# Six slots of raw weights instead of two in a decoder step's first block, on one Trainium2 core

## The chip, the cores and the metric

The kernel runs on one core of one Trainium2 chip. The metric is device time in microseconds (us), the median of several executions. The engines are named as in the profile: PE (TensorE, matmuls), PEld (its weight loads), DVE (VectorE), ACT (ScalarE), POOL (GpSimd) and SP (SyncE, which here only issues DMAs). ACT and POOL issue DMAs too.

## The reference

One inference step of a decoder block for a prompt of 2048 tokens and 8 decode tokens, all in f32, width 1024:

```python
mp, pc, pC, pn, pm = hybrid_mixer(rmsnorm(hp, g_mix[l]), zc, zC, zn, zm, w_in[l], ..., w_out[l], chunk_p)
hp = hp + mp
pk, pv = mem_kv(mem_prompt, g_mem[l], w_xkv[l])
hp = hp + cross_attn(rmsnorm(hp, g_cross[l]), pk, pv, w_xq[l], w_xo[l])
hp = hp + swiglu(rmsnorm(hp, g_ffn[l]), w_gu[l], w_down[l])
...
y_prompt = rmsnorm(hp, g_final)
```

`hybrid_mixer` is a large input projection, a short convolution, a recurrence over chunks (mLSTM) and an output projection; `mem_kv` makes keys and values of a memory of 256 rows; the FFN has width 2816. The 8 decode tokens take the same weights with states and caches of their own.

## The kernel before, in words

**Groups of weights.** All weights come as groups, tiles of 128x1024 f32 (512 KB), numbered in the order in which PE uses them. Groups 0 to 15 make the memory's keys and values from 256 columns. Groups 16 to 31 fold those keys and values into the query and output weights; the 32 results (the "made" tiles) go to DRAM as `made_d`. Then come five blocks of tokens, the first of 512, the others of 384, and each block uses the same 121 groups: a gate group, 4 groups for the output gate, 24 for the 4 heads (6 per head), 8 of `w_out`, 16 of cross-attention (from `made_d`), and 68 of the FFN. `G_LOW` = 32 + 121 = 153 is the end of the first block's groups.

**Raw groups.** A matmul is done in three passes over a high and a low part of both operands. Every group below `G_LOW` is raw: SP loads it from DRAM into a slot of `w_raw` (`NR` slots), ACT copies it, rounded, into the high half of a slot of `w_hl` (lines 998 and 1044, `NS` = 6 slots), and then the rest is computed by a subtraction, on DVE for groups 0 to 15 (line 1396) and on POOL for 16 to 152 (lines 477, 482). Of the first block's groups SP stores both halves (1 MB) to `split_d` (line 391); the four later blocks load these 1 MB tiles straight into `w_hl` and have no raw groups.

**The order of the work.** Each engine has its own program, in an order written out by hand, and counts on semaphores tie them together. SP loads the first `NR` groups at the start; after that the load of raw group n is issued when the subtraction of group n - NR is done, behind the store of group n - NR where there is one. ACT's copy of group n waits for its load, for PE to be done with group n - 6 (`group_done`), and for the store of group n - 6. In ACT's program this copy (`w_high`) stands between its other work (evictions from PSUM, exponentials, squares), so what stands behind it waits too.

**The place of the decode tokens' weights.** `dwt`, four slots of 128x1024, is a tensor of its own; POOL loads rows of weights into it in the third and fourth block (`decode_rows`), and PE uses them there for the 8 decode tokens.

Of the kernel before, what the change touches and what calls it, by code (L numbers as in the profile page):

```python
# [12 lines left out]
P = 128  # L13
D = 1024
# [27 lines left out]
G_MEM = 16  # L42
# [17 lines left out]
G_LOW = G_KV + G_BLK  # L60

NS = 6
NP = 3
NR = 2


C_BIN = 0
# [47 lines left out]
def gw(b, off):  # L115

    return G_KV + b * G_BLK + off
# [33 lines left out]
def raw(g):  # L151

    return g < G_LOW
# [8 lines left out]
OUT_COUNT, RAW, STORES, LOADS = [], [], [], []  # L162
# [12 lines left out]
def trunk(nc, x_blk, mem_x, w_kv, w_st, w_dec, cst_d, mats_d, st_conv, st_c, st_n, st_m, kd_d, vd_d,  # L175
          y, o_pconv, o_pc, o_pm, o_mk, o_mv, o_sconv, o_sc, o_sn, o_sm, rows_d, drow_d, vrow_d, qrow_d, prow_d, split_d, made_d):
    with ExitStack() as ctx:
        def sb(name, shape, dt=F32):
            return ctx.enter_context(nc.sbuf_tensor(name, shape, dt))

        def sem(name):
            return ctx.enter_context(nc.semaphore(name))
# [5 lines left out]
        act_lo = sb("act_lo", [P, KT, WM], F32R)  # L188
        w_raw = sb("w_raw", [P, NR, D])
        w_hl = sb("w_hl", [P, NS, 2, D], F32R)  # L190
        w_hi, w_lo = w_hl[:, :, 0, :], w_hl[:, :, 1, :]

        dwt = sb("dwt", [P, 4, D])
        big = sb("big", [P, 8200])
        work = sb("work", [P, 4128])
        V1 = P + 1
# [104 lines left out]
        def sems(names):  # L301
            return [sem(n) for n in names.split()]

        cst_loaded, mats_loaded, x0_loaded, xnext_loaded, x_loaded, set_up, dec_loaded = sems(
            "cst_loaded mats_loaded x0_loaded xnext_loaded x_loaded set_up dec_loaded")
        w_loaded = sems("w_loaded_0 w_loaded_1")
        memx_loaded = sems("memx_loaded_0 memx_loaded_1 memx_loaded_2 memx_loaded_3")

        w_hi_done, w_lo_kv, w_lo_done, group_done, out_a, out_v = sems(
            "w_hi_done w_lo_kv w_lo_done group_done out_a out_v")  # L310
# [59 lines left out]
        def _(sp):  # L370
            def weights(g):
                src = w_kv[g] if g < G_KV else w_st[g - G_KV]
                if attends(g):
                    src = made_d[g - gw(0, O_XQ)]
                i = RAW[g] - 1
                sp.dma_start(w_raw[:, i % NR, :], src).then_inc(w_loaded[i % NR], 16)

# [7 lines left out]
            sp.dma_start(cst[:], cst_d).then_inc(cst_loaded, 16)  # L385
            for g in range(NR):
                weights(g)
# [12 lines left out]
            raws = [g for g in range(G_LOW) if raw(g)]  # L400
            for i in range(NR, len(raws) + NR):
                g = raws[i - NR]

# [33 lines left out]
        def _(pool):  # L437
            def load_rows(b):

                n = tok(b) + BLK[b]  # L440
                pool.wait_ge(rows_stored, b * 32 + 32)
                for h in range(HEADS):
                    pool.dma_start(bc[:, h, 0:n], rows_d[h:h + 1, 0:n].to_broadcast([P, n])).then_inc(bc_loaded, 16)  # L443

            def load_x(b):

                after(pool, y_stored, b * 64)
                for k in range(0, KT, 4):
                    pool.dma_start(x[:, k:k + 4, 0:tok(b)],
                                  x_blk[b * KT + k:b * KT + k + 4, :, 0:tok(b)].rearrange("k p c -> p k c")).then_inc(x_loaded, 16)  # L450
                if b == DO:
                    pool.dma_start(x[:, :, DC:DC + NDEC],
                                  x_blk[DM * KT:DM * KT + KT, :, DC:DC + NDEC].rearrange("k p c -> p k c")).then_inc(x_loaded, 16)

            def load_next(b):

                w = w_mix(b + 1)
                pool.wait_ge(y_lo, b * 8 + 8)
                for k in range(0, KT, 4):
                    pool.dma_start(x_next[:, k:k + 4, 0:w],  # L460
                                  x_blk[(b + 1) * KT + k:(b + 1) * KT + k + 4, :, 0:w].rearrange("k p c -> p k c")).then_inc(xnext_loaded, 16)

            def store_y(b):
                w = w_ffn(b)
                for k in range(0, KT, 2):
                    pool.wait_ge(y_ready, b * 8 + k + 2)
                    pool.dma_start(y[b * KT + k:b * KT + k + 2, :, 0:w].rearrange("k p c -> p k c"),
                                  x[:, k:k + 2, 0:w]).then_inc(y_stored, 16)

            for g in range(G_MEM, G_LOW):  # L470
                if not raw(g):
                    continue
                pool.wait_ge(w_hi_done, RAW[g])
                raw_w, hi_w, lo_w = w_raw[:, (RAW[g] - 1) % NR, :], w_hi[:, g % NS, :], w_lo[:, g % NS, :]
                if g == gw(0, O_GATE):
# [17 lines left out]
            def decode_mixer():  # L493

                pool.wait_ge(drow_stored, 16)
                for h in range(HEADS):
                    pool.dma_start(dbc[:, h, :], drow_d[h:h + 1, :].to_broadcast([P, 24])).then_inc(dbc_loaded, 16)

            def decode_states():
                pool.wait_ge(o_lo, DM * 8 + 8)  # L500
                for h in range(HEADS):
                    pool.dma_start(c_dec[:, h * NDEC:(h + 1) * NDEC, :].rearrange("p t v -> p (t v)"),
                                   st_c[:, h * 1024:(h + 1) * 1024]).then_inc(c_loaded, 16)
                pool.wait_ge(vrow_stored, 16)
                rows = vrow_d.rearrange("(s h t) d -> s h (t d)", s=2, h=HEADS)
                for h in range(HEADS):

                    after(pool, dc_ready, 2 * h - 1)
                    pool.dma_start(k_bc.rearrange("p t d -> p (t d)"), rows[1, h:h + 1, :].to_broadcast([P, NDEC * P])).then_inc(vb_loaded, 16)
                    after(pool, dc_ready, 2 * h)  # L510
                    for i in range(2):
                        src = rows[0, h:h + 1, i * 512:(i + 1) * 512].rearrange("h (e c) -> h e c", c=64).to_broadcast([P, 8, 64])
                        pool.dma_start(q_bc[i], src).then_inc(qb_loaded, 16)
                pool.wait_ge(dc_ready, 2 * HEADS)
                pool.dma_start(o_sc, big[:, 4096:8192]).then_inc(dst_stored, 16)
                pool.dma_start(o_sn, dn).then_inc(dst_stored, 16)
                pool.wait_ge(dy_ready, 1)
                pool.dma_start(o_sconv, dcout.rearrange("p i h t -> p (i h t)")).then_inc(dst_stored, 16)
# [15 lines left out]
            def decode_rows(i):  # L534

                after(pool, dw_used, i - 3)
                pool.dma_start(dwt[:, i % 4, :], w_dec[i] if i < KT else w_kv[G_MEM + i]).then_inc(dw_loaded[i % 4], 16)

            def decode_caches():
                pool.wait_ge(o_lo, DO * 8 + 8)  # L540
                cache(0)
                cache(1)
                pool.wait_ge(qrow_stored, 16)
                for i in range(4 * NDEC):
                    if i == 2 * NDEC:
                        pool.wait_ge(prow_stored, 16)
                    piece_row(i)

                    if i % 2 == 0 and 4 <= i:
                        cache(i // 2)  # L550

            for b in range(1, NB):
                load_rows(b)
                if b == DM:
                    decode_mixer()
                store_y(b - 1)
                load_x(b)
                if b < NB - 1:
                    load_next(b)
                if b == DM:  # L560
                    decode_states()
                if b == DO:
                    for i in range(KT):
                        decode_rows(i)
                    decode_caches()

                    for i in range(4):
                        decode_rows(KT + i)
                if b == DX:
                    for i in range(4, KT):  # L570
                        decode_rows(KT + i)
# [1462 lines left out]
```

## Time and profile before

| | |
|---|---|
| median of 3 runs | 2984.13 us (2983.05 to 2984.96) |
| profiled execution, its own time | 2980.44 us |
| its span, first to last instruction | 2978.6 us |
| PE busy | 2892.0 us, 97% |
| DVE, ACT, POOL busy | 1177.9, 754.5, 427.9 us |
| moved by DMA | 801.14 MB, mean 269 GB/s |

A row of the timeline gives start, duration, engine, line, operation, output tile and inputs, and in brackets how long the engine had been idle and what released it. A window's row gives each engine's busy time, PE's granted clock as a share of full speed, the mean busy share of the 16 DMA engines, and what they moved.

### The profile page before, as it was taken

How to read it: one execution, taken by the hardware profiler on the slowest of the kernel's cores; microseconds unless marked ns; L12 is line 12 of the kernel's file. 1: busy time of each engine (PE TensorE's matmuls, PEld its weight loads, DVE VectorE, ACT ScalarE, POOL GpSimd, SP SyncE). 2: the span in 40 equal slices, each digit the busy share in tenths (PEclk: the TensorE clock that was granted, in tenths of full speed). 3: DMA queues.
4: the chain of work that ended last, by engine and by line, in shares of the span. 5: the costliest groups of instructions: out<-in, count | busy, mean ns of one | idle time of the engine just before them, and what ended most of it. 6: DMA issues, size and time to landing. Idle time of an engine off the chain costs nothing.

```text
span 2978.6 us, 38344 instructions
## 1 busy us (share of the span) xinstructions
PE 2892.0 (97%) x15739; PEld 2706.0 (91%) x15739; DVE 1177.9 (40%) x2240; ACT 754.5 (25%) x1472; POOL 427.9 (14%) x286
## 2 busy tenths in 40 slices
PE   7789999999999999999999999999999999999998
PEld 6667877888889999999997999998899999999998
DVE  5525546422553344323333456533332233332223
ACT  4433334322232231103222110222220123221001
POOL 0543343444420000000000102000000000000000
PEclk9999999999999999999999999999999999999999
DMA  5787686978977777877676789976666777567674
GB/s 185 235 322 265 221 306 225 315 277 280 315 268 277 257 277 278 301 266 289 249 283 253 286 343 371 363 272 247 217 250 244 265 264 277 219 251 249 253 267 178
DMA packets 143974, 801.14 MB, mean 269 GB/s; under 512 B 15949, under 2 KB 31693, under 8 KB 64057
## 3 DMA queue, kind: packets, MB, share of 16 engines
q1 hardware_dynamic: 112048, 719.10, 66.5%
q0 software_dynamic: 16208, 67.87, 6.5%
q10 hardware_dynamic: 15544, 11.72, 1.3%
q8 instruction: 126, 2.06, 0.3%
q14 instruction: 48, 0.39, 0.0%
HBM read 650.30 MB, written 148.33 MB: 268 GB/s over the span
## 4 chain that ended last, share of the span: by engine, by line
PE 85%; DMA 6%; DVE 2%; POOL 2%; ACT 2%; issue 2%; SPq 0%; ACTq 0%; DVEq 0%
PE gb L613 75%; DMA w_raw<-w_st 3%; PE gb L853 3%; POOL w_hl L482 2%; PE ta L853 2%; DMA w_raw<-w_kv 2%; ACT w_hl L998 1%; PE td L853 1%; DMA big<-kd_d 1%; DMA w_raw<-made_d 0%; PE ta L722 0%; PE gm L835 0%; DVE work L1550 0%; PE tb L733 0%; DVE w_hl L1396 0%
## 5 line engine op out<-in xcount | busy, mean ns | idle before, releaser
L613 PE MATMUL gb<-xn_hi,w_hl 128*128 128x384 f32 (+2 forms) x5800 | 1582.8, 349 | 4.4 <-DVE x L1639 1.4
L613 PEld LDWEIGHTS gb<-xn_hi,w_hl 128*128 128x128 f32 x5800 | 1061.0, 188 | 53.2 <-issue 5.3
L613 PE MATMUL gb<-xn_lo,w_hl 128*128 128x384 f32 (+2 forms) x2920 | 1011.9, 347 | 0.0
L613 PE MATMUL gb<-act_hi,w_hl 128*128 128x384 f32 (+3 forms) x3296 | 872.1, 344 | 22.2 <-DVE w_hl L1396 11.2
L613 PEld LDWEIGHTS gb<-act_hi,w_hl 128*128 128x128 f32 x3296 | 599.5, 189 | 55.9 <-DVE w_hl L1396 11.5
L613 PEld LDWEIGHTS gb<-xn_lo,w_hl 128*128 128x128 f32 x2920 | 548.9, 188 | 24.2 <-issue 0.5
L613 PE MATMUL gb<-act_lo,w_hl 128*128 128x384 f32 (+3 forms) x1648 | 564.1, 342 | 0.0
L482 POOL TENSOR_TENSOR w_hl<-w_raw,w_hl 128x1024 fp32r<-128x1024 f32 x136 | 330.2, 2433 | 495.2 <-ACT w_hl L998 495.2
L1447 DVE TENSOR_TENSOR work<-gb,r_res 128x384 f32<-128x384 f32 (+2 forms) x220 | 128.3, 585 | 555.4 <-PE gb L613 522.0
L613 PEld LDWEIGHTS gb<-act_lo,w_hl 128*128 128x128 f32 x1648 | 312.1, 189 | 12.3 <-issue 0.2
L1639 DVE TENSOR_TENSOR x<-x,gb 128x384 f32<-128x384 f32 (+2 forms) x200 | 115.4, 581 | 417.4 <-PE gb L613 414.1
L998 ACT ACTIVATE w_hl<-w_raw 128x1024 fp32r<-128x1024 f32 x147 | 154.6, 1057 | 390.9 <-DMA w_raw<-w_st 157.5
L1298 ACT ACTIVATE work<-work 128x384 f32<-128x384 f32 (+2 forms) x110 | 59.9, 545 | 514.9 <-DVE work L1447 514.8
L1301 ACT ACTIVATE act_hi<-work 128x384 fp32r<-128x384 f32 (+2 forms) x110 | 60.1, 546 | 333.0 <-DVE work L1866 333.0
L1218 ACT ACTIVATE work<-x 128x384 f32<-128x384 f32 (+2 forms) x120 | 65.6, 546 | 309.4 <-DVE x L1639 286.9
L1653 DVE TENSOR_TENSOR r_res<-r_res,work 128x384 f32<-128x384 f32 (+2 forms) x119 | 91.1, 766 | 68.5 <-ACT work L1218 67.0
L443 POOL DMA_DIRECT2D big<-rows_d x20 | 10.9, 551 | 658.5 <-DMA rows_d<-big 658.5
L1866 DVE TENSOR_TENSOR work<-work 128x384 f32<-128x384 f32 (+2 forms) x110 | 85.3, 775 | 28.1 <-ACT work L1298 17.5
L1108 ACT ACTIVATE big<-gb,cst 128x384 f32<-128x384 f32 (+1 forms) x80 | 48.5, 606 | 175.3 <-PE gb L613 173.9
L1549 DVE TENSOR_TENSOR work<-ta,big 128x128 f32<-128x128 f32 x64 | 18.6, 291 | 184.2 <-ACT work L1189 141.6
L1853 DVE TENSOR_TENSOR act_lo<-work,act_hi 128x384 fp32r<-128x384 f32 (+2 forms) x110 | 85.0, 773 | 12.4 <-ACT act_hi L1301 11.7
L853 PE MATMUL gb<-w_hl,xn_hi 128*128 128x512 f32 x240 | 78.0, 397 | 5.8 <-DVE x L1639 5.8
(303 smaller groups left out, 2071.0 us busy)
## 6 DMA issues: line engine op xcount, KB each, us to landing
w_hl<-split_d SPq DMA_DIRECT2D x484, 1024.0 KB, 5.0
split_d<-w_hl SPq DMA_DIRECT2D x121, 1024.0 KB, 5.0
w_raw<-w_st SPq DMA_DIRECT2D x105, 512.0 KB, 5.9
w_raw<-w_kv SPq DMA_DIRECT2D x32, 512.0 KB, 3.7
made_d<-big ACTq DMA_DIRECT2D x32, 256.0 KB, 4.0
w_raw<-made_d SPq DMA_DIRECT2D x16, 512.0 KB, 5.8
big<-kd_d POOLq DMA_DIRECT2D x8, 1024.0 KB, 10.8
big<-vd_d POOLq DMA_DIRECT2D x8, 1024.0 KB, 12.8
```

Source lines behind the costliest of these rows:

```text
L482: pool.tensor_tensor(lo_w, raw_w, hi_w.bitcast(F32), ALU.subtract).then_inc(w_lo_done, 1)
L613: mm = pe.matmul(gb[:, ps, 0:wd], a[:, s, k * P:(k + 1) * P], r[:, k, 0:wd], start=(first and k == ks[0] and i == 0), stop=(last and k == ...
L853: mm = pe.matmul(score_bank(p, t), a[:, kt, t * P:(t + 1) * P], r[:, g % NS, n * 512:n * 512 + 512], start=(kt == 0 and f == 0), stop=(kt ...
L998: act.activation(w_hi[:, n % NS, :], w_raw[:, i % NR, :], ACT.Copy).then_inc(w_hi_done, 1)
L1218: act.activation(sq_res[:, 0:wd], x[:, e, 0:wd], ACT.Square).then_inc(res_sq, 1)
L1298: act.activation(et[:, 0:W], gt[:, 0:W], ACT.Silu).then_inc(e_ffn, 1)
L1301: act.activation(act_hi[:, f, 0:W], ht[:, 0:W], ACT.Copy).then_inc(hid_hi, 1)
L1447: return lambda ps: v.tensor_tensor(dst[:, 0:wd], ps[:, 0:wd], r_res[:, 0:wd], ALU.mult)
L1639: return lambda ps: v.tensor_tensor(x[:, e, 0:wd], x[:, e, 0:wd], ps[:, 0:wd], ALU.add)
L1653: v.tensor_tensor(acc_res[:, 0:wd], acc_res[:, 0:wd], sq_res[:, 0:wd], ALU.add).then_inc(res_acc, 1)
L1853: v.tensor_tensor(act_lo[:, f, 0:W], ht[:, 0:W], act_hi[:, f, 0:W].bitcast(F32), ALU.subtract).then_inc(hid_lo, 1)
L1866: v.tensor_tensor(ht[:, 0:W], et[:, 0:W], ut[:, 0:W], ALU.mult).then_inc(h_ffn, 1)
```

## The change

`NR` goes from 2 to 6. The four new slots take no new memory: `dwt` becomes slots 2 to 5 of `w_raw`. Four more semaphores count the loads. In the third block (`DO`), ahead of the first load of decode rows, POOL waits until the last raw group has been subtracted.

```diff
-NR = 2
+NR = 6
...
-        dwt = sb("dwt", [P, 4, D])
+        dwt = w_raw[:, 2:6, :]
...
-        w_loaded = sems("w_loaded_0 w_loaded_1")
+        w_loaded = sems("w_loaded_0 w_loaded_1 w_loaded_2 w_loaded_3 w_loaded_4 w_loaded_5")
...
                 if b == DO:
+
+                    pool.wait_ge(w_lo_done, RAW[G_LOW - 1] - G_MEM)
                     for i in range(KT):
                         decode_rows(i)
```

SP's program at its start (`w_kv` holds groups 0 to 31, `w_st` those of the blocks, `split_d<-w_hl` are the stores), as a difference of before (-) and the changed kernel (+):

```order
 L385 DMA cst<-cst_d 128x96
-L376 DMA w_raw<-w_kv 128x1024 x2
+L376 DMA w_raw<-w_kv 128x1024 x6
 L388 DMA mats<-mats_d 128x896
-L376 DMA w_raw<-w_kv 128x1024 x30
-L376 DMA w_raw<-w_st 128x1024 x2
-L391 DMA split_d<-w_hl 128x2048
```

Six loads stand ahead of that of `mats` instead of two, and each later load stands four groups earlier against the stores: six loads of the first block's groups, instead of two, are issued before its first store.

SP's program where the raw groups end (`w_hl<-split_d` are the later blocks' loads):

```order
 L391 DMA split_d<-w_hl 128x2048
 L376 DMA w_raw<-w_st 128x1024
-L391 DMA split_d<-w_hl 128x2048 x2
+L391 DMA split_d<-w_hl 128x2048 x6
 L398 DMA w_hl<-split_d 128x2048 x484
```

The last six stores have no load between them, where before it was two. The instructions of PE, ACT, DVE and POOL keep their order.

## Rows read from the trace of the kernel before

**Rows 1.** The page: PE's busy time, and the chain that ended last

```profile
PE 2892.0 (97%) x15739; PEld 2706.0 (91%) x15739; DVE 1177.9 (40%) x2240; ACT 754.5 (25%) x1472; POOL 427.9 (14%) x286
...
PE gb L613 75%; DMA w_raw<-w_st 3%; PE gb L853 3%; POOL w_hl L482 2%; PE ta L853 2%; DMA w_raw<-w_kv 2%; ACT w_hl L998 1%; PE td L853 1%; DMA big<-kd_d 1%; DMA w_raw<-made_d 0%; PE ta L722 0%; PE gm L835 0%; DVE work L1550 0%; PE tb L733 0%; DVE w_hl L1396 0%
```

**Rows 2.** Windows: length, busy time of each engine, PEclk, DMA share, GB/s

```profile
0.00:32.00 32.00, 11.65 (x49) 10.36 (x50) 14.86 (x30) 13.60 (x23) 0.20 (x4) 0.79 0.73 245
32.00:77.00 45.00, 43.16 (x340) 41.27 (x339) 29.72 (x37) 21.89 (x31) 7.05 (x3) 1.00 0.43 142
77.00:117.00 40.00, 26.03 (x192) 24.88 (x192) 33.76 (x36) 20.12 (x34) 22.30 (x10) 0.96 0.62 204
117.00:157.00 40.00, 28.34 (x100) 21.57 (x101) 9.42 (x14) 15.00 (x19) 20.43 (x10) 0.83 0.90 299
157.00:230.00 73.00, 63.23 (x290) 52.21 (x289) 18.33 (x37) 26.31 (x36) 28.14 (x15) 0.95 0.85 308
230.00:380.00 150.00, 145.65 (x706) 121.20 (x705) 83.26 (x140) 57.78 (x117) 59.96 (x27) 1.00 0.70 249
380.00:410.00 30.00, 24.20 (x99) 19.28 (x98) 16.87 (x16) 12.20 (x16) 11.96 (x5) 0.94 0.87 331
460.00:850.00 390.00, 389.14 (x1713) 321.22 (x1712) 167.31 (x166) 123.72 (x161) 169.47 (x70) 1.00 0.82 282
```

**Rows 3.** ACT's timeline: copies of raw weights, with the idle time ahead

```profile
13.28 1.06 ACT L1044 ACTIVATE w_hl<-w_raw 128x1024 fp32r<-128x1024 f32 x1 [1.65 <-DMA w_raw<-w_kv]
15.87 1.06 ACT L1044 ACTIVATE w_hl<-w_raw 128x1024 fp32r<-128x1024 f32 x1 [0.83 <-DMA w_raw<-w_kv]
19.95 1.06 ACT L1044 ACTIVATE w_hl<-w_raw 128x1024 fp32r<-128x1024 f32 x1 [2.31 <-DMA w_raw<-w_kv]
25.85 1.06 ACT L1044 ACTIVATE w_hl<-w_raw 128x1024 fp32r<-128x1024 f32 x1 [4.14 <-DMA w_raw<-w_kv]
...
145.15 1.06 ACT L998 ACTIVATE w_hl<-w_raw 128x1024 fp32r<-128x1024 f32 x1 [4.96 <-DMA w_raw<-w_st]
150.56 1.06 ACT L998 ACTIVATE w_hl<-w_raw 128x1024 fp32r<-128x1024 f32 x1 [4.35 <-DMA w_raw<-w_st]
```

**Rows 4.** PE's timeline: matmuls ahead of which PE was idle

```profile
77.86 0.36 PE L660 MATMUL gb<-act_hi,w_hl 128*128 128x256 f32 x1 [0.87 <-DVE act_lo L1421]
80.86 0.38 PE L660 MATMUL gb<-act_hi,w_hl 128*128 128x256 f32 x1 [1.33 <-DVE work L1412]
84.96 0.38 PE L660 MATMUL gb<-act_hi,w_hl 128*128 128x256 f32 x1 [2.42 <-DVE work L1412]
89.49 0.36 PE L660 MATMUL gb<-act_hi,w_hl 128*128 128x256 f32 x1 [1.40 <-issue]
...
152.15 0.79 PE L678 MATMUL gb<-w_hl,act_hi 128*128 128x512 f32 x1 [7.25 <-ACT big L1083]
156.06 0.47 PE L613 MATMUL gb<-xn_hi,w_hl 128*128 128x512 f32 x1 [0.99 <-DVE big L1428]
```

**Rows 5.** Windows in which the granted clock was low

```profile
190.00:196.00 6.00, 5.33 (x17) 4.55 (x18) 0.21 (x1) 5.40 (x5) 3.79 (x5) 0.50 0.50 149
404.00:408.00 4.00, 3.70 (x9) 2.96 (x10) 2.61 (x3) 1.24 (x2) 2.15 (x1) 0.57 1.00 328
152.00:156.00 4.00, 2.93 (x6) 1.82 (x6) 0.83 (x2) 1.23 (x3) 2.06 (x1) 0.62 1.04 360
130.00:136.00 6.00, 5.28 (x16) 4.19 (x17) 0.69 (x1) 2.32 (x4) 3.42 (x2) 0.72 1.00 293
```

**Rows 6.** DMA issues from 10 to 20 us: count, KB each, us to landing

```profile
big<-x_blk ACTq DMA_DIRECT2D x1, 2048.0 KB, 12.6
```

**Rows 7.** Sources: ns min/median/max of DVE and POOL instructions

```profile
L1421 DVE TENSOR_TENSOR act_lo<-x,act_hi x8: 417/2405/2436, 62.5 to 85.4; 128x256 fp32r<-128x256 f32 x8
...
L1428 DVE COPY big<-gb x16: 675/684/693, 88.7 to 155.1; 128x512 f32<-128x512 f32 x16
...
L482 POOL TENSOR_TENSOR w_hl<-w_raw,w_hl x136: 2338/2395/2865, 67.5 to 840.4; 128x1024 fp32r<-128x1024 f32 x136
```

## The prediction

> **What bounds the kernel now.** The page comes first. PE is busy for 2892.0 of 2978.6 us, and the chain that ended last runs 75% through one matmul line; loads of `w_raw` hold 5% of that chain and POOL's subtraction 2% [rows 1]. So nearly everything is matmul work that the change leaves alone, and what it can move is PE's idle time and the time at a low clock. The windows say where these are [rows 2]. From 460 to 850 us, with raw groups still being loaded, stored and subtracted, PE is busy for 389.14 of 390 us: there two slots are enough. PE's idle time lies in front: 20.35 us up to 32, 1.84 up to 77, 13.97 up to 117, 11.66 up to 157, 9.77 up to 230, 4.35 up to 380 and 5.80 up to 410 us (each the length less PE's busy time).
>
> Next I asked what ACT waits for before it copies a raw group, since PE rarely waits for weights by name. In the opening ACT waited 1.65, 0.83, 2.31 and 4.14 us for the loads of groups 2 to 5, and later 4.96 and 4.35 us for two loads in a row; right after these two PE shows its longest gap, 7.25 us, released by ACT's line 1083, an eviction that stands behind the copies in ACT's program [rows 3, 4]. That is the pattern: a load comes late because its slot was released late, ACT stands at the copy, and PE waits for a bank, a row of exponentials or a residual tile that ACT would have delivered. After such a gap the clock drops: with a clock of 0.50 PE was busy for 5.33 us from 190 to 196 us [rows 5].
>
> **The change, stretch by stretch.** With six slots the load of group n is issued when group n - 6 is subtracted. ACT's copy of n waits in any case for PE to finish n - 6, some five groups after that subtraction. A group of 24 matmuls in the first block takes 389.14 us / 1713 x 24 = 5.45 us [rows 2], so a load gets about 25 us to land. The loads should then leave the chain, unless the queue is 25 us behind.
>
> Up to 32 us. The copies of groups 2 to 5 waited 1.65 + 0.83 + 2.31 + 4.14 = 8.93 us [rows 3]. All six loads are now issued at once, but they land one behind the other, and DVE needs some 2.1 us a group in this loop, so I take 8 us. Against it: ACT's load of the first block's `x` (2 MB) took 12.6 us [rows 6]; it will now be issued earlier, among more loads, and the group after this loop waits for it. I take 1 us back: **-7.0**. Bounds: 0, if `x` lands no earlier than before, and -8.9.
>
> 32 to 77 us. 1.84 us idle [rows 2], of which I take **-1.0**; bounds 0 and -1.8.
>
> 77 to 90 us. The first four gaps of the key stages (line 660) are 0.87 + 1.33 + 2.42 + 1.40 = 6.02 us [rows 4]. They come from DVE, which works through eight subtractions `act_lo` paced by ACT's copies, which in turn wait for loads. With the loads early these subtractions are done while PE is still on group 15: **-6.0**; bounds -2 (DVE is no faster by itself) and -6.
>
> 90 to 117 us. PE is idle for the other 13.97 - 6.02 = 7.95 us [rows 2, 4]. Here ACT does not wait for loads; DVE is busy for 33.76 of 40 us and is held up by POOL's pairs of subtractions. I take **0**; bounds 0 and -8, and +4 if POOL hits it harder.
>
> 117 to 157 us, the four value stages. 11.66 us idle, less 1 us that the evictions at the end cost anyway, and low clock: 5.28 us busy at 0.72 and 2.93 at 0.62 lose 1.5 + 1.1 us [rows 2, 5]. Of 13.3 I take **-13.0**; bounds -4 and -13.3. The lower one is for a saturated queue, see below.
>
> 157 to 230 us, the first block's opening and first head. 9.77 us idle, and half of 5.33 us at a clock of 0.50, 2.7 us: 12.5 [rows 2, 5]. Some of it is the real latency of the rows of gates, so **-11.0**; bounds -3 and -12.5.
>
> 230 to 380 us, the other heads: 4.35 us idle [rows 2], **-3.5**; bounds 0 and -4.3.
>
> 380 to 410 us, the way from `w_out` into cross-attention: 5.80 us idle, and 3.70 us busy at 0.57, 1.6 us [rows 2, 5]. Of 7.4 I take **-6.0**; bounds -1 and -7.4.
>
> From 410 us on: 0. The idle time there isn't behind loads, and PE is full from 460 us. POOL's new wait is for a count that POOL itself completed in the block before: 0, since POOL's own program has passed it. `dwt` in another place costs nothing. `mats` is loaded behind four more groups (2 MB), but its first user is the sum at the end of the opening: 0.
>
> Sum: 7.0 + 1.0 + 6.0 + 13.0 + 11.0 + 3.5 + 6.0 = 47.5 us. The profiled execution took 2980.4 us, so its like would take 2932.9. The median is 3.7 us above that execution; I carry the same offset: **2936.6 us, said as 2937**.
>
> **Is the DMA queue fast enough?** This speaks against the change most. From 117 to 157 us the DMA engines are busy for 0.90 of the time and move 299 GB/s, from 157 to 230 for 0.85 at 308 GB/s [rows 2]. I want to take 13 + 11 = 24 us out of these 113 us; idle DMA time in them is 0.10 x 40 + 0.15 x 73 = 15 us. But the queue no longer has to keep up: four groups (2 MB) come earlier, from a stretch with a share of 0.43, and that is 2 MB / 308 GB/s = 6.8 us less here; and a backlog of up to 25 us costs nothing. Together 15 + 6.8 = 21.8 us without any backlog, and 24 with 2 us of it. So I take the larger figure, but it is near the edge.
>
> In the opening the six loads share the DMA engines with ACT's loads. The Trainium skill, "DMA: Bandwidth & Descriptors", section "Queues, rings and completion order", says that a DMA engine takes turns between the queues that have work for it. By that rule `x` keeps half of the rate and lands about when it did, which is the 1 us above; if the queues were served in order of issue instead, it would land behind the loads. No row here shows six loads deep.
>
> **Rivals.**
>
> *The DMA engines are the bound from 117 to 230 us.* For it: shares of 0.90 and 0.85. Stores of 1 MB and loads of 0.5 MB stand in one queue, and the 2 MB of memory keys and values are now queued four groups sooner. If the loads are as late as before there, the terms of 13 and 11 us fall to their bounds, 4 and 3: 47.5 - 17 = 30.5 us, 2954. If even these vanish, 23.5 us and 2961. Against it: the 25 us.
>
> *DVE stays the bound.* If DVE paces everything up to 117 us, only the loads' 7 us in the opening and the value stages count, and if new gaps open in the heads as well, 30 us are left, 2954 again; it shares that case.
>
> *Slower: POOL's subtractions fall on DVE work that PE waits for.* DVE's `act_lo` subtraction takes 417 ns by itself and 2405 ns in the median, which is the length of POOL's own 2395 ns; a copy from PSUM never varies, 675 to 693 ns [rows 7]. So a DVE instruction can lose 2.0 us behind POOL. At present the pauses between POOL's subtractions are set by late loads; when ACT copies at once on `group_done`, each subtraction falls at a fixed place of PE's group. If that is the wrong place in all 121 groups, it costs 121 x 2.0 = 242 us less 47, some 3180 us; it decides from 24 groups on (47.5 / 2.0). Against it: from 460 to 850 us the copies already follow `group_done`, and PE loses 0.86 us in 390. The same is stated in the Trainium skill, "SBUF — State Buffer", section "Who interferes with whom": VectorE with two inputs in SBUF and GpSimd share a port that one of them holds for a whole instruction. The trace agrees, by the 417 and 2405 ns.
>
> *No change.* Each gap is replaced by another of the same length, since ACT's late work had a second cause as late as the load. That needs all seven terms to fail, 2984.
>
> *More than forecast.* All upper bounds, with the 8 us from 90 to 117: 8.9 + 1.8 + 6 + 8 + 13.3 + 12.5 + 4.3 + 7.4 = 62.2 us, 2922.
>
> **How the numbers follow.** The forecast, 40 to 56 us less (2928 to 2944): 0.55. The DMA bound, with DVE, 20 to 40 us less (2944 to 2964): 0.25. More than 56 us less: 0.10. Between 6 and 20 us less: 0.04. No change: 0.03. Slower: 0.03. About 0.2% (6 us) is what a measurement of this kernel can tell from no change. The range takes in the forecast, the "more" down to 2922 and the DMA case to 2960. That gives faster 0.94, same 0.03, slower 0.03.
>
> **What would show it.** In the profile of the changed kernel ACT's copies should wait for PE, hardly for DMA. The opening, over at 32 us before, should be over at about 25; the first value stage, at 117 us before, should begin at about 103; the first block's gate group, at 156.06 us before [rows 4], at about 129; and the FFN some 47 us sooner. The DMA share in the 100 us around the first block's start should come near 1, and a raw load should take longer to land without anyone waiting for it. The prediction is wrong if ACT still waits for `w_raw` around the gate group (DMA bound), if PE's gaps there are released by DVE lines with two SBUF inputs of 2.4 us (POOL), or if the key stages take as long from start to end as before and the value stages wait for ACT for another reason.

## The result and the profile after

The changed kernel takes 2945.97 us in the median (2943.5 to 2947.64, 4 runs) against 2983.59 before (2982.88 to 2984.96, 4 runs): a ratio of 0.9873 (95% interval 0.9856 to 0.989). Later, in the same rounds as three experiments, it came out at 0.9874 (0.9859 to 0.9889). Forecast were 2937 us and a range from 2922 to 2960. The profiled execution's span went from 2978.6 to 2941.7 us, 36.9 less where the sum had 47.5.

The page of the changed kernel, the lines that answer to [rows 1]; line numbers are up by two, so that 998 is now 1000, 1083 is 1085 and 1108 is 1110:

```profile
PE 2880.3 (98%) x15739; PEld 2700.8 (92%) x15739; DVE 1166.3 (40%) x2240; ACT 755.5 (26%) x1472; POOL 431.2 (15%) x286
...
PE gb L615 82%; PE gb L855 3%; PE ta L855 2%; DMA made_d<-big 1%; PE td L855 1%; DMA big<-kd_d 1%; PE gb L680 1%; DMA w_hl<-split_d 1%; DMA big<-x_blk 1%; PE ta L724 0%; PE gb L662 0%; PE gm L837 0%; DMA w_raw<-w_kv 0%; PE ta L789 0%; PE ta L883 0%
```

The loads of `w_raw` were 5% of the chain; the one row of them that is left rounds to 0%, and POOL's subtraction is not among the rows. In their place stands a store, `made_d<-big`, 1%. ACT's waits of the first 820 us in the changed kernel (line, what it waited for, us in total, times, longest):

```profile
ACT w_hl L1000 <- PE gb L615: 235.0, 69, 10.8
...
ACT big L1110 <- DMA made_d<-big: 17.4, 1, 17.4
```

The copies now wait for PE, as the prediction said they would, and one single wait of 17.4 us stands out. PE's timeline shows what it costs; these are all its gaps of about 1 us and more from 30 to 1700 us (behind them come two more, of 1.52 and 1.19 us):

```profile
30.58 0.55 PE L615 MATMUL gb<-act_hi,w_hl 128*128 128x256 f32 x1 [5.25 <-DVE x L1414]
86.63 0.36 PE L662 MATMUL gb<-act_hi,w_hl 128*128 128x256 f32 x1 [3.54 <-issue]
95.78 0.36 PE L662 MATMUL gb<-act_hi,w_hl 128*128 128x256 f32 x1 [1.68 <-issue]
104.65 0.77 PE L680 MATMUL gb<-w_hl,act_hi 128*128 128x512 f32 x1 [2.80 <-issue]
129.10 0.47 PE L615 MATMUL gb<-xn_hi,w_hl 128*128 128x512 f32 x1 [0.99 <-DVE big L1430]
145.92 0.47 PE L615 MATMUL gb<-xn_hi,w_hl 128*128 128x512 f32 x1 [2.04 <-DVE big L1468]
165.36 0.76 PE L615 MATMUL gb<-xn_hi,w_hl 128*128 128x512 f32 x1 [13.75 <-ACT big L1110]
423.36 0.66 PE L837 MATMUL gm<-mats,work 128*128 128x128 f32 x4 [3.23 <-DVE work L1702]
```

The row at 104.65 is the first value stage, that at 129.10 the gate group, and both come where they were forecast (103 and 129). The last one stands at 458.38 us before, with a gap of 3.22. Three gaps are new. At 30.58 PE waits for the load of `x`. At 145.92 it loses 2.04 us and at 165.36 another 13.75, together more than the value stages had gained. The gaps of 4.86, 2.23 and 2.68 us that stood between 190 and 218 us before are gone, as the prediction wanted. ACT's timeline ahead of the new gaps, in the changed kernel:

```profile
132.03 11.57 ACTq L1079 DMA_DIRECT2D made_d<-big  x1
132.88 1.04 ACT L1000 ACTIVATE w_hl<-w_raw 128x1024 fp32r<-128x1024 f32 x1
143.64 0.69 ACT L1115 ACTIVATE big<-gb,cst 128x512 f32<-128x512 f32 x1 [9.72 <-issue]
...
164.52 0.69 ACT L1110 ACTIVATE big<-gb,cst 128x512 f32<-128x512 f32 x1 [17.41 <-DMA made_d<-big]
```

ACT issues the last store of a made tile at 132.03, and the issue alone lasts 11.57 us: for 9.72 us ACT does nothing behind it, although the gate group is done; DVE gets the evicted gates only at 144.36, and the gap of 2.04 us follows. Then ACT waits 17.41 us more, since the output gates are evicted into the place of the made tiles and all their stores must have landed. The chain puts it in one row:

```profile
132.03 32.32 DMA made_d<-big
```

A store of 256 KB lands after 32.3 us; before, the longest took 10.7. The windows say why it could happen (columns as in [rows 2]):

```profile
32.00:72.00 40.00, 40.00 (x315) 39.52 (x315) 33.38 (x38) 21.62 (x31) 11.75 (x5) 0.95 0.58 184
72.00:105.00 33.00, 24.98 (x189) 24.40 (x189) 28.83 (x32) 17.54 (x30) 17.67 (x8) 0.94 0.67 220
105.00:130.00 25.00, 24.01 (x100) 19.42 (x100) 9.37 (x14) 13.52 (x18) 20.09 (x9) 0.95 0.98 321
130.00:170.00 40.00, 24.22 (x99) 19.29 (x98) 7.43 (x12) 10.84 (x15) 10.89 (x5) 0.83 0.83 321
170.00:210.00 40.00, 40.00 (x201) 33.65 (x200) 12.81 (x29) 17.65 (x30) 17.58 (x11) 1.00 0.89 336
```

From 105 to 130 us, the value stages, PE is busy for 24.01 of 25 us, and the DMA engines for 0.98 of the time. While that last store is under way, SP's queue (q1: weights, stores of the split weights, keys and values) and ACT's (q10: the made tiles) look so from 135 to 160 us (packets, MB, share of 16 engines); a packet of this view is one piece, here 512 bytes for the made tiles:

```profile
q1 hardware_dynamic: 1653, 9.14, 90.8%
q10 hardware_dynamic: 1644, 0.82, 11.2%
```

The two queues get through the same number of pieces, and SP's queue through eleven times the bytes. From 132 us to the landing ACT's queue moves 2238 pieces, as many as 4.4 made tiles have: the last store stood behind some three others, and each of their pieces let a large one pass.

### The profile page after: what moved, and what is told of

The parts are those of the page before. It is cut to its first block, busy times and chain, and to the rows that moved or that the text cites. A ratio compares the mean times of both kernels' runs of the same rounds, so it can differ in the third digit from the quotient of the medians.

```text
span 2941.7 us, 38344 instructions
## 1 busy us (share of the span) xinstructions
PE 2880.3 (98%) x15739; PEld 2700.8 (92%) x15739; DVE 1166.3 (40%) x2240; ACT 755.5 (26%) x1472; POOL 431.2 (15%) x286
## 4 chain that ended last, share of the span: by engine, by line
PE 94%; DMA 3%; DVE 1%; issue 0%; ACT 0%; ACTq 0%; DVEq 0%; SPq 0%
PE gb L615 82%; PE gb L855 3%; PE ta L855 2%; DMA made_d<-big 1%; PE td L855 1%; DMA big<-kd_d 1%; PE gb L680 1%; DMA w_hl<-split_d 1%; DMA big<-x_blk 1%; PE ta L724 0%; PE gb L662 0%; PE gm L837 0%; DMA w_raw<-w_kv 0%; PE ta L789 0%; PE ta L883 0%
## 5 line engine op out<-in xcount | busy, mean ns | idle before, releaser
L615 PE MATMUL gb<-xn_hi,w_hl 128*128 128x384 f32 (+2 forms) x5800 | 1583.1, 349 | 19.5 <-ACT big L1110 13.7
L1868 DVE TENSOR_TENSOR work<-work 128x384 f32<-128x384 f32 (+2 forms) x110 | 66.4, 603 | 16.2 <-ACT work L1300 4.8
```

What stands on the lines that cost most here:

```text
L615: mm = pe.matmul(gb[:, ps, 0:wd], a[:, s, k * P:(k + 1) * P], r[:, k, 0:wd], start=(first and k == ks[0] and i == 0), stop=(last and k == ...
L1868: v.tensor_tensor(ht[:, 0:W], et[:, 0:W], ut[:, 0:W], ALU.mult).then_inc(h_ffn, 1)
```

## The experiments

All ratios are to the kernel before. Unless said otherwise, an edit is made to the changed kernel.

| run | edit | median us | ratio (95%) |
|---|---|---|---|
| e1 | keys and values stored 4 groups later | 2934.49 | 0.9847 (0.9832 to 0.9862) |
| e2 | wait for made tiles slot by slot | 2942.88 | 0.9874 (0.986 to 0.9889) |
| e3 | `x` loaded two steps earlier | 2943.32 | 0.9878 (0.9862 to 0.9895) |
| e4 | made tiles in rows of 2 KB | 2935.59 | 0.9849 (0.9834 to 0.9864) |
| e5 | four slots | 2946.31 | 0.9877 (0.986 to 0.9893) |
| e6 | three slots | 2944.24 | 0.9871 (0.9857 to 0.9886) |
| e7 | e1 and e4 | 2932.19 | 0.9829 (0.9814 to 0.9844) |
| e8 | two slots, rows of 2 KB | 2982.29 | 0.9993 (0.9984 to 1.0003) |
| e9 | none (six slots again) | 2945.8 | 0.9874 (0.9859 to 0.9889) |
| e10 | e4, keys and values 10 groups later | 2941.47 | 0.9859 (0.9842 to 0.9875) |
| e11 | e10 and e3, four slots | 2940.0 | 0.9855 (0.984 to 0.987) |
| e12 | e10 and e3, three slots | 2946.7 | 0.9877 (0.9863 to 0.9892) |

The kernel before had medians of 2980.17 us beside e1 to e4, 2983.41 beside e5 to e8 and 2983.36 beside e9 to e12, so ratios are compared, not times.

**e1, keys and values later.** In the kernel SP issues these two stores (1 MB each) with the load of the first block's group 6. With six slots that load stands four groups earlier in the work, and so do the stores: at 122.59 us, ahead of the last made tiles.

```diff
-                if off == 6:
+                if off == 10:
```

> The changed kernel (six slots) with one edit: the stores of the memory keys and values (2 MB) are issued four groups later, behind the same subtraction as in the kernel before. The changed kernel took 2946 us; its profile shows ACT waiting 17.4 us for the last stores of the made tiles, and PE losing 13.75 us behind that. Theory A (bytes): those 2 MB stand in front of the made tiles' stores; without them the last of these lands 2 MB / 380 GB/s = 5.5 us sooner, and the time falls to about 2940.5. Theory B (turns): the made tiles' stores go out in pieces of 512 bytes and get one piece's turn for each piece of 4 or 8 KB of a full SP queue; what fills that queue does not matter, weights only take the place of the 2 MB: 2944 to 2949, the gap stays above 11 us.

The longest landing of a made store fell from 32.3 to 20.6 us, PE's gap from 13.75 to 3.69. By the ratios it is 0.26% faster, 7.8 us; by the spans 2941.7 - 2937.4 = 4.3 us. The rows side with the ratios: PE's last gap stands at 415.26 us, 8.1 sooner than in the changed kernel. Theory A's 5.5 us are somewhat small, for the time and for the landing (11.7 us sooner). Theory B is wrong in saying that what fills the queue doesn't matter. Its turns are there all the same: from 130 to 140 us each of the two queues moves some 660 pieces, and when SP's queue runs low, from 140 to 145, ACT's gets 1566 pieces through against 210.

**e4, rows of 2 KB.**

```diff
                 if attends(g):
-                    src = made_d[g - gw(0, O_XQ)]
...
+                    m = g - gw(0, O_XQ)
+                    src = made_d[m]
+                    if m >= KT:
+                        c0 = (m - KT) * P
+                        src = made_d[KT:2 * KT, :, c0:c0 + P].rearrange("k p c -> p k c")
+                        dst = dst.rearrange("p (k c) -> p k c", k=KT)
...
-                    kt, m0 = 2 * h + j // 2, KT + j % 2 * 4
-                    dst = made_d[m0:m0 + 4, :, kt * P:(kt + 1) * P].rearrange("m p c -> p m c")
-                    src = made[:, i % 8, :].rearrange("p (m c) -> p m c", m=4)
+                    kt = 2 * h + j // 2
+                    dst, src = made_d[KT + kt, :, j % 2 * 512:j % 2 * 512 + 512], made[:, i % 8, :]
```

> The changed kernel with one edit: the 16 made tiles of the value half are stored in rows of 2 KB instead of pieces of 512 bytes, at another place of the same DRAM tensor, and the 8 groups of the output weights gather pieces of 512 bytes when SP loads them 200 us later. The bytes are the same. Theory B (turns): a store needs a quarter of the turns; the longest landing falls from 32.3 us to under 12, the longest issue on ACT from 11.57 us to under 3, the gap of 13.75 us goes: about 2931 us, less 0 to 3 us that the gathering loads may cost. Theory A (bytes): the queue is as long as before: 2944 to 2949.

The stores of the made tiles in the changed kernel and in e4 (ns min/median/max of the issue, us min/median/max to landing):

```profile
L1079 ACTq DMA_DIRECT2D made_d<-big x32: 366/520/11569, 73.6 to 132.0; - x32
...
DMA to landing us min/median/max: 2.4/5.7/32.3
```

```profile
L1084 ACTq DMA_DIRECT2D made_d<-big x32: 326/520/1321, 73.7 to 129.6; - x32
...
DMA to landing us min/median/max: 2.4/5.7/12.8
```

The same bytes, landed in 12.8 us at most; the long issue is down to 1.32 us, ACT's wait is gone, and so is PE's gap of 13.75 us. Theory A can't explain that. Nor can DMA time saved: ACT's queue from 105 to 165 us, in the changed kernel and in e4 (packets, MB, share of 16 engines):

```profile
q10 hardware_dynamic: 9264, 4.98, 27.6%
```

```profile
q10 hardware_dynamic: 3136, 4.99, 22.4%
```

5.2% of 60 us are 3.1 us, where the longest landing fell by 19.5. The pieces waited for their turns, as the equal counts of the two queues above say. Both theories are needed: small pieces get through a full queue of large ones slowly (B), and the 2 MB make that queue longer (A). The time fell less than forecast, to 0.9849 (7.5 us by the spans, 15 forecast), in the main because a new gap of 5.51 us came at the first head: the gaps of 2.04 and 13.75 us less this one are 10.3 us, and PE's last gap, at 412.74, stands 10.6 us sooner.

**e2, waits slot by slot.** The wait for the stores is spread, three slots ahead of three evictions and five ahead of the store of the gates' rows.

```diff
-                if b == 0:
-                    for slot_stored in pre_stored:
-                        act.wait_ge(slot_stored, 16 * (NPRE // 8))
                 for h in range(HEADS):
+                    if b == 0 and h < HEADS - 1:
+                        act.wait_ge(pre_stored[h], 16 * (NPRE // 8))
...
+                        if b == 0:
+                            for slot_stored in pre_stored[HEADS - 1:]:
+                                act.wait_ge(slot_stored, 16 * (NPRE // 8))
```

> The changed kernel with one edit: ACT waits for the stores of the made tiles slot by slot, where it first writes over that slot (one slot ahead of each of the first three output-gate evictions, the other five ahead of the store of the rows), not for all eight at the first eviction. Theory (this wait holds PE): the gap of 13.75 us ahead of a matmul of the output-gate groups goes, and with it about 1 us of low clock: about 2931 us. Rival (the loss moves): the made stores are as late as before, ACT is held a little later by the same landing, and PE loses 8 us or more at the rows of gates or the head's first chunk: 2940 or more.

The rival came true. The gap of 13.75 us became two, of 3.50 us and, at the first head, 5.47 us; the one of 2.04 us is still there, with 1.80. PE's last gap stands 5.0 us sooner, but the ratio is that of the changed kernel. So moving the wait is worth little, and nothing that the times can tell; that the stores are late is what costs.

**e3, `x` earlier.**

```diff
-                if k == 3:
+                if k == 1:
```

> The changed kernel with one edit: ACT issues the load of the first block's x (2 MB) two steps earlier in the opening loop (about 10 us instead of 14 us). In the changed kernel it landed at 30.0 us and PE stood 5.25 us for it. Theory (the load shares the DMA engines with twelve loads of weights that are not yet needed; it gets its half from the moment it is issued): it lands some 4 us sooner, the gap falls to about 1 us, 2942 us. Rival (the DMA engines are full from 4 to 28 us, so nothing is won: the weights of the opening loop come later instead): 2945 to 2948.

The ratio didn't move: the rival. The load was issued 4.3 us earlier and landed 1.2 us earlier, at 28.8 us, and PE goes on at 29.39 us instead of 30.58, less than the times can tell. The gap itself, 4.17 against 5.25 us, says little, since the changed kernel shows 3.90 in e9. The DMA engines moved 377 GB/s from 5 to 30 us in the changed kernel, twelve loads of weights and `x` among them; that an earlier issue then only changes the order is argued, not shown.

**e5 and e6, four and three slots** (the tensor keeps its six, so `dwt` stays where it is).

```diff
-NR = 6
+NR = 4
...
-        w_raw = sb("w_raw", [P, NR, D])
+        w_raw = sb("w_raw", [P, 6, D])
```

> The changed kernel with NR = 4: the same tensor of six slots, of which raw weights use four. Theory (the gain comes from loads that are issued early enough, the loss from a queue that is full around the gate group): four slots give a load some 15 us, enough in the opening and in the heads, and the first block's loads and the 2 MB of keys and values are queued two groups later. The gaps in front (opening, key stages, value stages) close as with six, and the wait for the made tiles' stores is shorter: the same as six slots or up to 6 us faster (ratio to before 0.985 to 0.9875). Rival (each slot counts, the loads need the depth of six at the saturated place): between before and six slots, ratio 0.990 to 0.994.

> The changed kernel with NR = 3. A load of 512 KB lands in 3.6 to 4 us when the queue is empty, and a key or value group takes 2.9 us, a group of the first block 5.4 us. Theory (most late loads were late by 2 to 6 us, one group's time): three slots already give two thirds of the gain, ratio 0.990 to 0.992, and ACT still waits for loads around the gate group. Rival (three slots are enough everywhere): the same as four slots. Rival (depth counts, not one more slot): under a third of the gain, 0.996 or more.

Four slots do what six do, by the first theory. Three do too, 0.9871, against the theory that depth or at least a fourth slot is needed. In e6 PE's gap for `x` is 1.41 us, not 5.25, but little is won by it: `x` lands at 29.5 us instead of 30.0, and the opening loop ends later (ACT's line 1024 at 25.26 us, not 22.50), so that PE comes to the gap later. The price is 1.91 and 1.17 us in the value stages, where ACT waits for loads again (17 times for 47.3 us up to 850 us, mostly hidden). The wait for the made tiles is still there, 14.2 us of ACT, and costs PE 10.59 us. As long as this wait stands, one slot more than two gives all that four more give; e12 below shows that it doesn't stay so.

**e7, both edits.**

> The changed kernel with both edits that helped alone: rows of 2 KB for the value half's made tiles (7.5 us by the spans) and the 2 MB of keys and values issued four groups later (4 us by the spans, about 7 by the medians). In the run with rows of 2 KB the first gap moved to the first head, 5.5 us, behind the rows of gates that come back through DRAM (a load of 258 KB took 10.9 us there). Theory (both edits attack one queue, and what is left is that gap): the gap shrinks to 2 us or less, about 4 us more than the rows alone: ratio 0.983 to 0.984. Rival (the 2 MB are paid later, the same bytes at another place of a saturated stretch): the same as the rows alone, 0.985.

At 0.9829 it has the lowest ratio of all, 13 us under the changed kernel (0.9874 - 0.9829 = 0.45%), though its interval still overlaps those of e1 and e4. The gap at the first head is 4.37 us, not under 2. DVE's row in e7 shows what is late there, the rows of gates that come back from DRAM:

```profile
174.31 0.69 DVE L1520 TENSOR_TENSOR big<-mats,big 128x512 f32<-128x512 f32 x1 [15.90 <-DMA big<-rows_d]
```

**e8, two slots with rows of 2 KB** (the edit of e4, in the kernel before).

> The kernel before (two slots) with the rows of 2 KB for the value half's made tiles alone. Before, the stores of the made tiles took at most 10.7 us to land and ACT waited 1.1 us for them. Theory (the small pieces only hurt behind a queue that six slots keep full): 0 to 3 us faster, within 0.1% of before. Rival (512-byte pieces cost DMA time that any kernel of this form pays in the stretch that is 0.90 to 0.97 full): 5 us or more faster, as much as with six slots.

The same time as before. The small pieces cost nothing that the times can tell until another queue is kept full: the longest landing is 9.8 us here and was 10.7.

**e9 to e12.** e9 is the changed kernel again; the others carry the rows of 2 KB and have the keys and values moved behind the subtraction of the first block's group 10 (`off == 16`, 14 and 13 for six, four and three slots). e11 and e12 have the earlier `x` too.

> The changed kernel itself, on the same chip and in the same rounds as the next three. All theories: ratio to before 0.986 to 0.989.

> Six slots, rows of 2 KB for the value half's made tiles, and the 2 MB of keys and values issued ten groups later than in the changed kernel (six later than in the run that had both edits, ratio 0.9829). There PE still lost 4.4 us at the first head, where the gates' rows come back through DRAM behind a full queue. Theory (that queue is full of the 2 MB's bytes): moved past the rows they leave the gap at 2 us or less, ratio 0.981 to 0.982. Rival (the stores and loads of weights alone fill the queue there): the gap stays, 0.982 to 0.984.

> Four slots, the same two edits (keys and values behind the same subtraction as in the run before this one), and the load of x two steps earlier. Fewer loads stand in the queues: the opening's wait for x falls from 4 to 5 us to 1 or 2, and the rows' loads wait less. Theory (a short lead is enough and a long queue only hurts): 2 to 5 us faster than six slots with the same edits, ratio 0.980 to 0.9815. Rival (depth makes no difference either way): the same as six slots, 0.981 to 0.983.

> As the run before it with three slots. Theory: with the made tiles' stores out of the way three slots are as good as four, within 2 us. Rival (in the saturated stretch ACT waits for loads again, up to 7 us each, as three slots alone showed): 3 to 8 us slower than four slots.

All three have higher ratios than e7 (for e10 and e11 the intervals just overlap with its), and for a reason that none of the theories had. DVE in e10:

```profile
180.45 0.06 DVE L1508 MEMSET work<- 128x2 f32 x1 [38.32 <-DMA o_mv<-work]
```

DVE reuses the place of the memory values and waits until they are stored. Issued at 168.56 us, that store holds DVE, and PE loses 10.51 us at the first head in e10, 12.64 in e11 and 8.94 in e12. In e7 DVE waits 13.1 us for the same store, but that is over at 154.50, before the rows come. The theory of e10 was right as far as it went: the rows of gates, loads of 258 KB, land in 5.1 us in the median where e7 has 9.8. The gain is hidden behind the other wait.

Four slots against six (e11, e10: 2940.0 and 2941.47 us, ranges that overlap) is left open by that. In the opening e11 has no gap for `x` over 1 us, the only run with four or more slots where that is so, and one of 2.07 us for a subtraction of weights instead. Three slots against four is not open: e12's rival came true, 2946.7 against 2940.0 us in the same rounds, with no overlap. PE loses 1.15 and 4.19 us in the value stages and 3.64 and 1.35 us in the opening, where e6, without the earlier `x`, shows nothing over 1 us from 20 us on but the gap for `x`. For these stores of keys and values, four groups are a good delay and ten too many.

## Why the prediction was right where it was, and where it was not

Shifts of the same rows between the two profiles, against the terms. PE ends the last group ahead of the key stages at 71.49 us after, where it was 76.99 (77.86 less its gap of 0.87); the value stages and the gate are in the rows; ACT's squares at the ends of heads 1 and 4 moved from 230.41 to 208.56 and from 348.99 to 321.88, and the last gap from 458.38 to 423.36.

| stretch before, us | forecast | measured | how |
|---|---|---|---|
| 0 to 77 | -8.0 | -5.5 | 71.49 - 76.99 |
| 77 to 117 | -6.0 | -6.9 | 104.65 - 117.05 = -12.4, less -5.5 |
| 117 to 157 | -13.0 | -14.6 | 129.10 - 156.06 = -27.0, less -12.4 |
| 157 to 230 | -11.0 | +5.1 | 208.56 - 230.41 = -21.9, less -27.0 |
| 230 to 380 | -3.5 | -5.2 | 321.88 - 348.99 = -27.1, less -21.9 |
| 380 to 458 | -6.0 | -7.9 | 423.36 - 458.38 = -35.0, less -27.1 |
| from 458 on | 0 | -1.9 | -36.9, less -35.0 |

**Right.** The mechanism: late loads made ACT late, and ACT made PE late. ACT no longer waits for weights but for 1.5 us in the opening, the longest landing of a raw load went from 11.5 to 20.7 us without anyone waiting for it, and five of seven stretches come out at or above their terms. Up to the gate group the sum had 27.0 us and the trace has 27.0, though its first term is 2.5 too large. The last row is not to be read: behind the last gap the fourteen profiles take from 2518.3 to 2523.4 us, and no run says why.

**The step that failed** is the term for 157 to 230 us, -11.0 where it was +5.1: 16 us, more than the whole miss of 10.6. Its bound was -3, so even the DMA rival, as priced, was too mild. "Is the DMA queue fast enough?" asked whether the bytes fit and what a late weight would cost. It allowed a backlog of 25 us because no load of weights was needed sooner. But the same DMA engines also carry stores that somebody does wait for: the made tiles, in pieces of 512 bytes, whose place ACT must have free at the gate group, 27 us sooner than before. A backlog that costs the weights nothing costs these everything. e4 shows it (the gap goes with the pieces), e1 shows the part that the 2 MB play, and that these would be issued four groups sooner had been written down as a rival's argument without asking what stands behind them. e2 shows that it is far more the landing than the place of the wait.

That the time still came within 9 us of the forecast, and in the range, is in part luck: the failed term is off by 16.1 us, and the other six give back 5.5 in sum. It is also 37.6 us less than before, in the band from 20 to 40 that had a chance of 0.25 for the DMA bound, not in the one from 40 to 56 with 0.55; the number fell to the rival, whose mechanism it isn't.

**Too small a price** was the 1 us that I took back for `x`. The opening loop itself ends 10.1 us sooner (ACT's line 1022, 32.57 us, now at 22.50), more than the 8 forecast; then PE stands 5.25 us for `x`. That load was issued at 15.97 us before and landed 12.6 later, at some 28.6; now it is issued at 14.07 and lands at 30.0, so it is later, not earlier, and as long as it is, the loop's gain beyond some 5 us can't be had. With four slots and the earlier issue (e11) it has landed by 27.8 us, and PE reaches the gap of 3.54 us in the key stages 2.7 us sooner (83.93 against 86.63).

**The rivals.** The DMA rival named the right resource and the wrong victim: it expected late weights. The rate itself was not the bound. The window from 130 to 170 us of e7, where the stores of the made tiles hold nobody:

```profile
130.00:170.00 40.00, 40.00 (x182) 33.26 (x181) 7.73 (x13) 19.08 (x23) 21.03 (x13) 1.00 1.01 391
```

PE is busy throughout at 391 GB/s. The prediction's idle DMA time was also counted too low: it took shares of 0.90 and 0.85 at 299 and 308 GB/s as nearly full, but a share is time, and small pieces take more of it for each byte (from 105 to 165 us, 4.98 MB take 27.6% in pieces of 512 bytes and 4.99 MB take 22.4% in e4). POOL's subtractions did not turn up: DVE's `act_lo` takes 2422 ns in the median (2405 before), and no gap of PE is released by it. The key stages keep their gaps of 3.54, 1.68 and 2.80 us, as the term of 0 for 90 to 117 us said. That DVE sets them, busy for 28.83 of 33 us from 72 to 105, is argued: the profile gives no releaser for them. The forecast's 25 us of lead held (20.7 us at most were needed) and was beside the point: three slots give the same time while the made tiles are late.

**Open.** The two largest gaps left in e7 are the 3.95 us for `x` and the 4.37 us at the first head. The first is under 1 us in e11, at a price elsewhere in the opening; the second was not cured. What four or three slots give with the keys and values four groups later, and whether another place for the memory values would free e10, was not tried. That e1's spans give 4.3 us, its medians 7.8 and its rows 8.1 comes from the part behind the last gap, which was 3.8 us longer in e1's profile; why it varies stays open.

## What to carry to other kernels

When prefetch is made deeper, list every transfer that shares the DMA engines with it and ask of each who waits for it: a backlog that the prefetched data can bear can still hold up a small store whose buffer is needed. Transfers in small pieces suffer first, so give them long rows and put the gather on a side where nobody waits. Settle the depth last: here one slot more did as much as four while another wait stood behind it, and with that wait cured three slots were 6.7 us slower than four (e12 against e11).

## What the runs showed of the hardware that was not expected

- An engine can be held by its own DMA issue. ACT's issue of a 256 KB store in 512-byte pieces took 11.57 us with the DMA engines full (both queues together 102% from 135 to 160 us), against 520 ns in the median, and ACT's next instruction stood 9.72 us. With rows of 2 KB the longest such issue took 1.32 us. It happens to SP as well: in e7 its issue of the memory values (1 MB), right behind that of the keys, took 11.90 us.
- Two busy queues take turns by the piece, whatever its size: 1653 pieces of SP's queue against 1644 of ACT's from 135 to 160 us in the changed kernel, for 9.14 and 0.82 MB, and in e7, with rows of 2 KB, 329 against 330 from 132 to 138 us. So a store in small pieces is slow beside a full queue of large ones: 256 KB in 512-byte pieces took up to 32.3 us to land, in 2 KB rows up to 12.8 us, with 3.1 us of DMA time between them. The Trainium skill, "DMA: Bandwidth & Descriptors", section "Queues, rings and completion order", says that a DMA engine takes turns between its queues by the packet; the trace agrees by the equal counts. The page's packet holds several descriptors, and whether a piece counted here is one such packet no run shows.
- The DMA engines moved 377 GB/s from 5 to 30 us, and 391 from 130 to 170 us in e7, at shares of 0.98 and 1.01, well above the 299 and 308 of the stretches that the prediction took as nearly full [rows 2].
